# Two attention layers of a four-layer block: output projections computed tile by tile, and new orders around the attention loops

## What is computed

```python
x = x + rmsnorm(nsa_mixer(rmsnorm(x, g0), ...), p0)     # "nsa": sparse, two softmax branches + compressed keys
x = x + rmsnorm(diff_mixer(rmsnorm(x, g1), ...), p1)    # "diff": p1 - lambda * p2, per-head rmsnorm
x = ple(x + mixer_na(rmsnorm(x, g2), ...))              # "na": neighbourhood attention, then a gated layer
x = ple(x + mixer_mla(rmsnorm(x, g3), ...))             # "mla": latent attention, then a gated layer
# each mixer: q, k, v, z = u @ w_in ; o = softmax(q k^T + bias) v ; y = (o * silu(z)) @ w_out
```

## Time and profile before

| | |
|---|---|
| median of 3 runs | 1464.06 us (1461.59 to 1464.49) |
| the profiled execution's own time | 1463.27 us |
| its span | 1461.5 us |
| PE busy | 1373.1 us (94%), 7818 matmuls and transposes |
| POOL busy | 780.9 us (53%) |
| ACT busy | 716.3 us (49%) |
| DVE busy | 621.6 us (43%) |
| granted PE clock, mean | 0.985 |

### The profile page before, as it was taken

How to read it: one execution, slowest core, us unless ns; L and a number is a source line. 1 busy time by engine, 2 the same in 40 slices (tenths; PEclk the granted TensorE clock), 3 DMA queues, 4 the chain that set the end, 5 groups by cost and what they waited for, 6 DMA issues and landing times.

```text
span 1461.5 us, 20933 instructions
## 1 busy us (share of the span) xinstructions
PE 1373.1 (94%) x7818; PEld 1125.8 (77%) x7818; DVE 621.6 (43%) x1606; ACT 716.3 (49%) x1533; POOL 780.9 (53%) x729
## 2 busy tenths in 40 slices
PE   6999999998989999998999999889999999999997
PEld 5887877777878888776778887678878886778785
DVE  3322178886250011883420013962341145887144
ACT  4244278886342323773423234963443354787252
POOL 5355266666554534474753353886456334566652
PEclk9999999999999999889999999999999999999999
DMA  6233210000443231212343233324225221001521
GB/s 238 88 116 115 92 56 27 31 30 32 156 141 119 87 116 58 73 44 91 140 129 131 87 110 118 120 89 161 101 93 196 98 87 59 1 1 59 187 87 58
DMA packets 27876, 139.57 MB, mean 95 GB/s; under 512 B 3328, under 2 KB 3712, under 8 KB 16128
## 3 DMA queue, kind: packets, MB, share of 16 engines
q1 hardware_dynamic: 14112, 98.57, 18.7%
q10 hardware_dynamic: 13664, 39.66, 7.9%
HBM read 129.83 MB, written 8.39 MB: 95 GB/s over the span
## 4 chain that ended last, share of the span: by engine, by line
PE 71%; POOL 11%; DVE 9%; ACT 5%; issue 2%; DMA 1%; ACTq 0%; POOLq 0%; SPq 0%; DVEq 0%
PE psum L393 57%; POOL w_lo L348 3%; POOL w_free L1342 3%; PE psum L1183 3%; PE psum L1164 2%; PE psum L1136 2%; DVE w_free L1232 2%; PE psum L877 2%; DVE u_lo L1245 2%; POOL split L1359 1%; ACT w_hi L339 1%; DVE arena L746 1%; ACT u_hi L1285 1%; PE psum L1149 1%; POOL split L1355 1%
## 5 line engine op out<-in xcount | busy, mean ns | idle before, releaser
L348 POOL TENSOR_TENSOR w_lo<-w_raw,w_hi 128x2048 fp32r<-128x2048 f32 (+2 forms) x118 | 427.0, 3632 | 431.8 <-ACT w_hi L339 431.0
L393 PE MATMUL psum<-u_lo,w_hi 128*128 128x512 f32 (+1 forms) x712 | 279.8, 393 | 0.9 <-DVE arena L1942 0.9
L393 PE MATMUL psum<-u_hi,w_lo 128*128 128x512 f32 (+1 forms) x712 | 277.3, 389 | 0.0
L393 PE MATMUL psum<-u_hi,w_hi 128*128 128x512 f32 (+1 forms) x712 | 277.3, 389 | 0.0
L339 ACT ACTIVATE w_hi<-w_raw 128x2048 fp32r<-128x2048 f32 (+1 forms) x93 | 172.9, 1859 | 155.0 <-DMA w_raw<-in_weights 101.8
L393 PE MATMUL psum<-w_hi,split 128*128 128x512 f32 x608 | 195.7, 394 | 6.0 <-POOL w_lo L348 4.3
L794 ACT ACTIVATE w_free<-w_free,neg_max 128x256 f32<-128x256 f32 (+3 forms) x320 | 183.6, 580 | 12.5 <-DVE neg_max L916 7.4
L393 PEld LDWEIGHTS psum<-u_lo,w_hi 128*128 128x128 f32 (+1 forms) x712 | 133.2, 187 | 30.3 <-POOL w_lo L348 1.3
L393 PEld LDWEIGHTS psum<-u_hi,w_hi 128*128 128x128 f32 (+1 forms) x712 | 133.2, 187 | 28.8
L393 PEld LDWEIGHTS psum<-u_hi,w_lo 128*128 128x128 f32 (+1 forms) x712 | 133.2, 187 | 27.3
L393 PE MATMUL psum<-w_hi,u_lo 128*128 128x512 f32 (+2 forms) x352 | 135.8, 386 | 10.0 <-DVE u_lo L752 7.6
(11 more groups left out here) (193 smaller groups left out, 2194.0 us busy)
## 6 DMA issues: line engine op xcount, KB each, us to landing
w_raw<-in_weights SPq DMA_DIRECT2D x90, 1024.0 KB, 4.8
x<-x_scratch ACTq DMA_DIRECT2D x12, 512.0 KB, 6.7
gain<-in_gains ACTq DMA_DIRECT2D x10, 512.0 KB, 4.6
gain<-in_strips ACTq DMA_DIRECT2D x16, 256.0 KB, 2.9
spare<-in_strips ACTq DMA_DIRECT2D x16, 256.0 KB, 2.9
x_scratch<-x ACTq DMA_DIRECT2D x16, 256.0 KB, 4.2
gain<-in_near ACTq DMA_DIRECT2D x8, 512.0 KB, 4.5
w_raw<-in_near ACTq DMA_DIRECT2D x8, 512.0 KB, 3.7
```

What stands on the lines that cost most here:

```text
L348: low = nc.gpsimd.tensor_tensor(w_lo[b][:, c], w_raw[b][:, c], w_hi[b][:, c].bitcast(F32), ALU.subtract)
L393: mm = nc.tensor.matmul(dst, lhs, rhs, start=(a == 0 and k == 0 and (wl, ul) == (0, 1)), stop=(a + 1 == u and k + 1 == nk and (wl, ul) == ...
```

## The change

It has seven parts; they are the same for the nsa and diff layers where both have the code.

1. `project_by_tile`: block 1 of `nsa_out` and `diff_out` is run with j outside and a inside, so each bank is done after its own 24 matmuls; it needs both units from the second product on. Tiles 0 and 1 of the next layer are turned within its products (a = 0, j = 2) and (0, 3), and the next projection uses `TWO_TO_TURN` (tiles 2 and 3 within (0,0) and (0,2)).
2. `chain_scalar`, `chain_pool`, `chain_vector`: new orders. ACT loads x after it has split unit +3; POOL's pieces of the next projection's first unit stand behind waits for `chain_summed` and `chain_normed`, that of its second unit, whole, behind the last root; DVE normalises a tile right after its sum.
3. ACT splits unit +2 of all four output projections before it waits for the last gated group, not after it and after issuing the loads of x.
4. `gated_half`: the second half (a = 1) of block 0 of `diff_out` runs chunks 0 to 2 of banks 0 and 1 before chunk 3, the one that needs the last gated group.
5. `LOW_STEPS`: POOL's eight pieces of unit `diff_out` +1 go to steps 12, 15, 16, 19, 20, 23, 24, 27.
6. `Flow(..., shift=0)` for nsa: `pair_tensor` starts at i = 0, so S(i), S(i+1) are the two steps of one pair, then T(i-3), V, T(i-2); V comes one step later.
7. In the last turns of nsa the first output product stands after V(29), the second after S/T of i = 66, the last two at the end.

```diff
-        nsa_flow = Flow("nsa", branched_steps(HEADS // 2), 2)
+        nsa_flow = Flow("nsa", branched_steps(HEADS // 2), 2, shift=0)
...
+        def gated_half(pe, f):
+
+            run = RUNS[f.name + "_out"]
+            pe.wait_ge(w_ready, run["unit"] + 2)
+            for j, chunks, last in ((0, (0, 1, 2), False), (1, (0, 1, 2), False), (0, (3,), True), (1, (3,), True),
+                                    (2, None, True), (3, None, True)):
+                mm = products(pe, run, 0, 1, j, gated_by=f, chunks=chunks)
+                if last:
+                    mm.then_inc(bank_done, 1)
...
+        TWO_TO_TURN = ((0, 0, 2), (0, 1, None), (0, 2, 3), (0, 3, None), (1, 0, None), (1, 1, None), (1, 2, None), (1, 3, None))
...
+        def project_by_tile(pe, name, gated_by, between):
+
+            run = RUNS[name]
+            for j in range(NT):
+                for a in range(2):
+                    pe.wait_ge(w_ready, run["unit"] + 2 + a + 1)
+                    if a == 0:
+                        wait_bank(pe, run, 1, j)
+                    mm = products(pe, run, 1, a, j, gated_by=gated_by, between=between.get((a, j)))
+                    if a == 0 and j == 3:
+                        mm.then_inc(w_used, 1)
+                mm.then_inc(bank_done, 1)
...
-        def chain_scalar(act, c, name):
-
-            split_next(act, name, 0, 0)
-            for j in range(NT):
+        def load_x(act, source):
+            for t in range(NT):
+                act.dma_start(x[:, t * D:(t + 1) * D], source[t * P:(t + 1) * P]).then_inc(x_back, 16)
+
+        def chain_scalar(act, c, name, source):
+
+            square_y(act, c, name, 0, 0)
+            split_next(act, name, 0, 1)
+            load_x(act, source)
+            for j in range(1, NT):
                 square_y(act, c, name, 0, j)
-            split_next(act, name, 0, 1)
+            square_y(act, c, name, 1, 0)
             split_next(act, name, 1, 0)
-            square_y(act, c, name, 1, 0)
             square_x(act, c, 0)
             square_y(act, c, name, 1, 1)
+            high_tile(act, c, 0)
+            square_x(act, c, 1)
             square_y(act, c, name, 1, 2)
-            square_x(act, c, 1)
-            high_tile(act, c, 0)
+            high_tile(act, c, 1)
+            square_x(act, c, 2)
             square_y(act, c, name, 1, 3)
+            high_tile(act, c, 2)
+            square_x(act, c, 3)
             split_next(act, name, 1, 1)
-            square_x(act, c, 2)
-            high_tile(act, c, 1)
-            square_x(act, c, 3)
-            high_tile(act, c, 2)
             high_tile(act, c, 3)
...
-            split_low(pool, n + 2)
             root_y(pool, c, 0)
+            pool.wait_ge(chain_summed, c.n - NT + 1)
+            split_low(pool, n + 2, 0)
             root_x(pool, c, 0)
             root_y(pool, c, 1)
-            root_y(pool, c, 2)
+            pool.wait_ge(chain_summed, c.n - NT + 2)
+            split_low(pool, n + 2, 1)
             root_x(pool, c, 1)
-            root_y(pool, c, 3)
-            split_low(pool, n + 3, 0)
-            split_low(pool, n + 3, 1)
-            root_x(pool, c, 2)
-            split_low(pool, n + 3, 2)
-            root_x(pool, c, 3)
-            split_low(pool, n + 3, 3)
+            pool.wait_ge(chain_normed, c.n + 2)
+            split_low(pool, n + 2, 2)
+            split_low(pool, n + 2, 3)
+            for t in (2, 3):
+                root_y(pool, c, t)
+                root_x(pool, c, t)
+            split_low(pool, n + 3)
...
             take_y(dve, c, 1, 0)
             add_y(dve, c, name, 0)
+            norm_tile(dve, c, 0)
             take_y(dve, c, 1, 1)
-            norm_tile(dve, c, 0)
             add_y(dve, c, name, 1)
-            take_y(dve, c, 1, 2)
             low_tile(dve, c, 0)
             norm_tile(dve, c, 1)
+            take_y(dve, c, 1, 2)
             add_y(dve, c, name, 2)
+            low_tile(dve, c, 1)
+            norm_tile(dve, c, 2)
             take_y(dve, c, 1, 3)
             add_y(dve, c, name, 3)
-            low_tile(dve, c, 1)
-            norm_tile(dve, c, 2)
+            low_tile(dve, c, 2)
             norm_tile(dve, c, 3)
-            low_tile(dve, c, 2)
             low_tile(dve, c, 3)
...
+        LOW_STEPS = (12, 15, 16, 19, 20, 23, 24, 27)
...
-                if 12 <= i < 20:
-                    split_low(pool, RUNS["diff_out"]["unit"] + 1, i - 12, 8)
+                if i in LOW_STEPS:
+                    split_low(pool, RUNS["diff_out"]["unit"] + 1, LOW_STEPS.index(i), 8)
...
-            for i in range(-1, f.steps + LAG + 1, 2):
+            for i in range(-f.shift, f.steps + LAG + 2 - f.shift, 2):
...
-                if i == f.steps + 1:
-                    first_output(pe, f, 0)
+                if i == f.steps + 2 - f.shift:
+                    first_output(pe, f, 0 if f.shift else 1)
...
-                d = (i - LAG) // 2 - 1
+                d = (i + f.shift) // 2 - LAG
                 if d >= 0:
                     values(d, 0)
                     values(d, 1)
+                if i == f.steps and not f.shift:
+                    first_output(pe, f, 0)
                 if 0 <= i + 1 - LAG < f.steps:
                     turn(i + 1 - LAG)
-                if i == f.steps + 1:
+                if i == f.steps + 2 - f.shift and f.shift:
                     first_output(pe, f, 1)
...
         def residual_scalar(act, c, nth):
 
             name, proj = ("na_out", "mla_out")[nth], RUNS[f"ple{nth}_proj"]
-            split_next(act, name, 0, 0)
             act.wait_ge(p_in, 16 * (nth + 1))
...
-            project_tensor(pe, "diff_out", gated_by=diff_flow, only=(0,), begun=True)
-            project_tensor(pe, "diff_out", gated_by=diff_flow, only=(1,), between={(1, 1, 3): lambda: turn_tile(pe, na_chain, 0)})
-            project_turning(pe, na_chain, "na_v", INTERLEAVED)
+            gated_half(pe, diff_flow)
+            project_by_tile(pe, "diff_out", diff_flow, {(0, 2): lambda: turn_tile(pe, na_chain, 0), (0, 3): lambda: turn_tile(pe, na_chain, 1)})
+            project_turning(pe, na_chain, "na_v", TWO_TO_TURN)
...
+            split_next(act, "mla_out", 0, 0)
             act.wait_ge(mla_flow.gated, 2 * KC)
             load_gain(act, 9)
-            for t in range(NT):
-                act.dma_start(x[:, t * D:(t + 1) * D], x_scratch[t * P:(t + 1) * P]).then_inc(x_back, 16)
+            load_x(act, x_scratch)
             load_p(act, 1)
```

More of the change, by code:

```diff
@@ L371, in products @@
             b = SLOT[run["unit"] + a + (0 if wide else u * i)]
-            for k in range(nk):
+            for k in chunks or range(nk):
                 if between is not None and k == nk // 2:
@@ L2015, in _ @@
             project_tensor(pe, "nsa_out", gated_by=nsa_flow, only=(0,), begun=True)
-            project_tensor(pe, "nsa_out", gated_by=nsa_flow, only=(1,),
-                           between={(1, 1, 3): lambda: turn_tile(pe, diff_chain, 0)})
-            project_turning(pe, diff_chain, "diff_v", INTERLEAVED)
+            project_by_tile(pe, "nsa_out", nsa_flow, {(0, 2): lambda: turn_tile(pe, diff_chain, 0), (0, 3): lambda: turn_tile(pe, diff_chain, 1)})
+            project_turning(pe, diff_chain, "diff_v", TWO_TO_TURN)
             project_tensor(pe, "diff_v", only=(1,))
@@ L2113, in _ @@
             load_gain(act, 4)
+            split_next(act, "diff_out", 0, 0)
             act.wait_ge(diff_flow.gated, 2 * KC)
             load_gain(act, 3)
-            for t in range(NT):
-                act.dma_start(x[:, t * D:(t + 1) * D], x_scratch[t * P:(t + 1) * P]).then_inc(x_back, 16)
-            chain_scalar(act, na_chain, "diff_out")
+            chain_scalar(act, na_chain, "diff_out", x_scratch)
             for r in range(8):
```

16 lines of the change are left out of this document (7 added, 9 removed).

## The result

The changed kernel took 1445.28 us, median of 6 runs (1441.95 to 1453.16), against 1462.35 us (1461.45 to 1464.49, 6 runs) for the kernel before: a ratio of 0.9886, 95% interval 0.9859 to 0.9914. The prediction said 1444.0. The profiled execution took 1441.95 us with a span of 1440.1, that of before 1463.27 with 1461.5.

What follows compares the result with a forecast made beforehand. PE, busy for 94% of the span, was taken as the bound, so only its waits, with drain and slow clock, could be gained. Terms of 6.0 + 9.4 + 2.8 + 1.7 = 19.9 us gave 1444 us, range 1437 to 1454.

Steps and rivals of the forecast that it cites:

- The chains: Between layers after nsa and diff: 1.2 to 2.0 us lost instead of 6.6, 4.7 us gained in each, 9.4 together.
- The nsa flow: Loop over pairs of heads in nsa: new step order saves 0.8 us per pair, 6.0 us over 7.5 pairs.
- rival (a): nsa flow gives nothing, savings at step s5 come back as waits before other scores and transposes: 1450 us; chance 0.18.
- layout: nsa's new order laid out step by step with row durations for two pairs of heads: 17.9 us per pair against 19.03.
- leg two: nsa loop, from transposes of step s5 to the next of s2: PE the bound, 12.26 us falls to 11.5.
- leg one: nsa loop, from transposes of step s2 to those of s5: not set by PE, 6.77 us before, keeps 6.4 to 6.8.
- The end of diff: End of diff: waits for the last gated group (1.8 us) and unit +2's low part go, 2.8 us together.
- rival (b): Both chains: POOL's whole weight unit gets ahead of tile 3's norm, turn 3.6 us late in each: 1451 us; chance 0.08.
- mla_out: In mla_out: the 1.44 us wait, taken as one for unit +2's low part, goes with 0.2 of drain, 1.7 us.
- The clock in diff: diff flow, part 5's spread pieces: nothing taken, with 6 us of gain and 3 us of loss kept as ends.
- rival (c): diff flow: the denser lists keep the clock up, worth 6 us: 1438 us; chance 0.07.
- Rival (d): nsa turns: PE waits for DVE before each second score, 0.9 us per turn: 1479 us, sign turns from 0.65; chance 0.03.

Runs made afterwards that it cites:

- moving the two pieces: Changed kernel with POOL's two weight pieces put behind the first root of tile 2 in both chains: 1445.79 us, 0.9886 of before.
- doubled pieces: Kernel before with POOL's work on unit diff_out +1 doubled, a zero added in place ahead of each of eight pieces: 1468.25 us, 1.0027 of before.
- the variant with the two ends: Changed kernel with a semaphore per tile of x in mla_out and nsa's first output product ahead of the transposes that waited 1.90 us: 1447.33 us.

## Why the prediction was right, and where it was not

**The chains** (parts 1 and 2, 9.4 us forecast): right in size, place and remainder. 4.7 and 4.8 us were found; the wait left over is 1.32 us on tile 2 (1.2 forecast), none is over 0.3 elsewhere, and moving the two pieces removes it. The account of a tile as its bank plus 6.8 us holds: behind nsa the squares of tile 0 start at 383.63 and its norm ends at 390.46. Wrong inside it was the split of the loss: 1.7 us for the clock were none, and the chain's lateness had all of the 6.6. (The terms as written, 4.2, 0.3 and 1.7, add up to 6.2; at full clock the waits are 2.41, 1.93 and 1.50 us and, with 0.2 of drain each, 6.4.)

**The nsa flow** (part 6, 6.0 us): right in direction, mis-sized by 5 us, and the time that rival (a) had for the flow is what came, near nothing. Its mechanism, new waits in place of the old, isn't: in a pair of heads PE's idle time fell from 1.96 to 1.27 us, while its own busy time rose from 17.07 to 17.35. The step that failed is the change from rows to layout. From the rows I had 0.05 us less work and one wait of 0.30 us, 0.35 us for leg two, and 6.4 to 6.8 for leg one; found were 0.36 and 6.72. The layout then promised a further 0.4 us in each leg, and none of it came. 0.41 us per pair make 2.9 over seven intervals. The first T(s5) comes 0.6 later after the first score, and from the last T(s5) to block 1 it takes 30.1 us (348.19 to 378.28) instead of 28.8 (351.47 to 380.30), since more of the flow's work now stands behind it: 1.0 us is left. The text itself named what held leg one, `gate_out` ahead of the scaling of s5; it then didn't ask what moving that would give: 4.6 us on the kernel after and, at like clock, some 3.7 on that of before.

**Part 7** (nothing): the products themselves are neutral, but the output product now stands behind the transposes that wait 1.90 us. With it ahead of them the stretch is 2.2 us shorter. "Before and after them the PE list is full" was the step; at the end of a flow the order of a wait and the work that could cover it counts.

**The end of diff** (2.8): 2.5 found, PE without a wait from the second half of block 0 to the first turn. Unit +3 and the whole unit behind tile 3's root, rival (b), did no harm: the norm of tile 3 goes at 408.78 with 1.28 us, 0.9 us ahead of POOL's unit.

**mla_out** (1.7): none. The row named POOL's `w_lo` as what PE waited for, and that was 6 us early after the change; the additions behind the loads of x were as late before the change as after it. The term failed on the question asked of every other stall and not of this one: what is late next.

**The clock in diff** (0, with 6 us as an end and as rival (c)): 5.9 us in the profiled run. Each us at the lower level costs PE some 0.3 us there, since waits of the flow absorb the rest (outside its busy time PE has 8.9 us in it with no fall and 6.5 in the kernel before): 80.0 to 80.1 us from first to last score with no fall, 82.4 with 10.2 us of it, 85.8 to 86.3 with 20.4, 88.5 and 89.4 with 27.3, 91.9 with 37.5. Why it falls less often is only partly settled. Both the dense chains and the spread pieces are needed for a mean clock of 0.992: with either alone it is 0.986 to 0.987, with neither 0.986. Falls within the old chains are 0.002 of it in the profile of before, 0.001 or nothing in those of the four other kernels with old chains. And doubled pieces take it to 0.981. But the mean clock differs from run to run of one kernel, six runs carry the case without part 5, and the variant with the two ends, which has both parts, had 27.3 us of it. That more work of POOL in those steps acts through the clock is shown, by the doubled pieces; why spreading the pieces does nothing without the new chains is open.

**Rival (d)**, waits for DVE before the second score, didn't come: 1.7 us in eight places over the whole flow, the longest 0.4. Its price had a slip: if the 6.0 us of the flow don't come either, 13.9 us of gain are left, and 0.43 us per turn would have turned the sign, not 0.65.

## What to carry to other kernels

Where a wait stands on an engine's list, look first for a step that could stand behind the awaited one; here two lines in POOL's list gave more than a new order of the whole loop. Take a loop's gain from rows (work removed, waits that must go) and give a layout's surplus little weight when three engines are over 80% busy. For each stall removed, name the second-latest input of every instruction in its neighbourhood; and compare kernels at equal granted clock, or stretch by stretch.

## What the runs showed of the hardware

A spell at 1.2 GHz costs what PE's idle time doesn't absorb. Where a chain on other engines sets the time it is nothing (54.00 us with 3.4 us at the lower level and with none). In the diff flow it is 0.23 to 0.34 us for each us. Where PE has few waits it is nearly half: 1.5 us for 3.4 in plain products (19.36 against 17.87), in the first turns of nsa, and in the new chain behind its first turn, 1.4 in mla. The mean clock differs between runs of the same program, 0.986 to 0.995 in the ten of the kernel after, and with it goes most of the spread of 1442 to 1453 us; in which stretch the falls of the unprofiled runs lie isn't on record. I hadn't expected either; my prediction took half of each such spell as lost, which is right only where PE is full.
